# Joining the context and x feed-forward stages, and four unused products behind the last transposes of a stage

## The reference, cut to what matters

```python
def ffn_half(s, shift, scale, gate, g_pre, g_post, w_in, w_out):
    h = swiglu_2(modulate(rmsnorm_2(s, g_pre), shift, scale), w_in, w_out)
    return s + 0.5 * gate * rmsnorm_2(h, g_post)

xs = ffn_half(xs, mod_x[0], mod_x[1], mod_x[2], g[0], g[1], w_ff_in[l, 0], w_ff_out[l, 0])
cs = ffn_half(cs, mod_c[0], mod_c[1], mod_c[2], g[0], g[1], w_ff_in[l, 0], w_ff_out[l, 0])
hx = modulate(rmsnorm_2(xs, g[2]), mod_x[3], mod_x[4])
hc = modulate(rmsnorm_2(cs, g[2]), mod_c[3], mod_c[4])
```

## Time and profile before

| what | value |
|---|---|
| median of three runs | 2783.65 us |
| the profiled execution, its own time | 2785.72 us |
| span of the profile | 2783.7 us |
| PE matmul busy | 2589.7 us, 93% of the span |
| PE weight load, DVE, ACT, POOL busy | 74%, 66%, 52%, 3% |
| mean granted TensorE clock | 0.959 of full speed |
| `ff0c` and `ff0x` together, first L791 to the last L819's end | 1679.1 to 2083.6 us |

### The profile page before, as it was taken

The page is one execution under the profiler, slowest core; times in us unless marked ns, Lnnn a source line. Parts: engine busy times, 40 slices in busy tenths (PEclk is TensorE's granted clock), DMA queues, the critical chain, the costliest instruction groups (busy, mean ns, idle before and its releaser), DMA issues.

```text
span 2783.7 us, 34461 instructions
## 1 busy us (share of the span) xinstructions
PE 2589.7 (93%) x11943; PEld 2048.8 (74%) x11943; DVE 1823.6 (66%) x1799; ACT 1454.5 (52%) x1670; POOL 73.1 (3%) x46
## 2 busy tenths in 40 slices
PE   6889998877999999999999989999999989888998
PEld 5567886656878787888878777877874768667786
DVE  5445445556888989888888975445534565666544
ACT  4354444354767777776767764434432333446443
POOL 0000000041000000000000000000000000020000
PEclk9889999888999999999999999999999999999999
DMA  5756552657999999999999994554534325315551
GB/s 188 242 190 219 181 190 67 239 190 247 367 345 353 349 351 351 352 349 345 356 335 367 335 348 142 192 167 143 190 106 135 116 91 170 106 61 169 194 186 55
DMA packets 445869, 631.64 MB, mean 227 GB/s; under 512 B 17656, under 2 KB 345752, under 8 KB 445592
## 3 DMA queue, kind: packets, MB, share of 16 engines
q1 hardware_dynamic: 444920, 627.36, 67.1%
q0 software_dynamic: 864, 3.15, 0.3%
HBM read 629.40 MB, written 1.05 MB: 226 GB/s over the span
## 4 chain that ended last, share of the span: by engine, by line
PE 85%; DVE 8%; ACT 4%; issue 2%; DMA 1%; SPq 0%; DVEq 0%; ACTq 0%
PE ps L791 38%; PE ps L819 20%; PE ps L1145 5%; PE ps L725 5%; PE ps L1165 2%; PE ps L1077 2%; PE ps L913 1%; PE ps L804 1%; PE ps L853 1%; ACT Bs L1507 1%; DVE small L2508 1%; PE ps L1136 1%; PE ps L866 1%; ACT As L1459 1%; DVE Bs L2033 1%
## 5 line engine op out<-in xcount | busy, mean ns | idle before, releaser
L1996 DVE TENSOR_TENSOR As<-ringA,As 128x2048 fp32r<-128x2048 f32 x318 | 728.9, 2292 | 217.4 <-ACT As L1459 208.3
L791 PE MATMUL ps<-As,xgs 128*128 128x512 f32 x2688 | 665.9, 397 | 3.2 <-DVE As L1996 1.8
L819 PE MATMUL ps<-Bs,hds 128*128 128x512 f32 x2472 | 601.1, 396 | 24.0 <-DVE hds L2011 24.0
L1459 ACT ACTIVATE As<-ringA 128x2048 fp32r<-128x2048 f32 x318 | 608.0, 1912 | 20.4 <-DMA ringA<-in_dense_w_up 9.3
L791 PEld LDWEIGHTS ps<-As,xgs 128*128 128x128 f32 x2688 | 495.0, 188 | 113.1 <-issue 10.7
L819 PEld LDWEIGHTS ps<-Bs,hds 128*128 128x128 f32 x2472 | 472.6, 192 | 128.1 <-DVE hds L2011 23.1
L791 PE MATMUL ps<-As,xs 128*128 128x512 f32 x2160 | 522.9, 399 | 15.0 <-DVE hh L2027 8.1
L791 PEld LDWEIGHTS ps<-As,xs 128*128 128x128 f32 x2160 | 408.9, 191 | 104.9 <-DVE hh L2027 9.4
L2033 DVE TENSOR_TENSOR Bs<-ringB,Bs 128x2048 fp32r<-128x2048 f32 x159 | 364.5, 2292 | 154.6 <-ACT Bs L1507 154.0
L1507 ACT ACTIVATE Bs<-ringB 128x2048 fp32r<-128x2048 f32 x159 | 304.9, 1918 | 205.0 <-PE ps L819 204.8
L1480 ACT ACTIVATE hds<-ps 128x256 fp32r<-128x256 f32 x206 | 74.0, 383 | 322.8 <-PE ps L804 288.0
(11 more groups left out here) (342 smaller groups left out, 2419.9 us busy)
## 6 DMA issues: line engine op xcount, KB each, us to landing
ringA<-in_moe_w_gate SPq DMA_DIRECT2D x224, 512.0 KB, 4.5
ringA<-in_moe_w_up SPq DMA_DIRECT2D x224, 512.0 KB, 5.6
ringB<-in_moe_w_down SPq DMA_DIRECT2D x112, 1024.0 KB, 6.3
ringA<-in_w_ff_in SPq DMA_DIRECT2D x132, 512.0 KB, 4.7
ringA<-in_w_in SPq DMA_DIRECT2D x56, 1024.0 KB, 5.3
ringA<-in_w_ada SPq DMA_DIRECT2D x36, 1024.0 KB, 5.4
ringB<-in_w_ff_out SPq DMA_DIRECT2D x33, 1024.0 KB, 4.9
ringA<-in_dense_w_gate SPq DMA_DIRECT2D x28, 512.0 KB, 3.6
```

The source lines that it names most:

```text
L791: m = mm(ps[:, bank, :], lhs(l, tt, k), As[:, h, r, k % 4, :], start=k == 0 and n == 0, stop=k == KC - 1 and n == 2)
L819: m = mm(ps[:, 4 + 2 * tt + half, :], hds[:, buf, l, q, :], Bs[:, q, r, half * 512:(half + 1) * 512], start=first and q == 0 and n == 0, s ...
L1459: A(As[:, h, 0, :, :], ringA[:, (p["a"] + u) % 2, 4 * h:4 * h + 4, :], ACT.Copy).then_inc(A_high, 1)
L1996: V.tensor_tensor(As[:, h, 1, :, :], ringA[:, (p["a"] + u) % 2, 4 * h:4 * h + 4, :], f32(As[:, h, 0, :, :]), ALU.subtract).then_inc(A_spli ...
```

## The change

1. `ff0c` no longer drains (`drains=False`) and `ff0x` no longer leads (`leads=False`): the `turn` and `down` of the last context block are made inside the first block of `ff0x`, as between any two blocks.
2. The `norm("ff0x")` goes. x is squared and scaled tile by tile before the first block of `ff0c`, as before that block now; its transposes are made by the PE at the ends of blocks 1 and 2 of `ff0c` (eight each, one tile, L697's helper `turn_rows`, banks 2 and 3). ACT evacuates bank 2 ahead of its blocks 2 and 3, DVE bank 3 behind its blocks 1 and 2, four 128x128 instructions each. The PE waits for both (`x_rows_out`) before the `turn` of blocks 2 and 3. Ahead of ACT's block 3 and behind DVE's block 3, x is split into `hcTR` and `hTR`, which `ff0x` reads in the place of `xs`.
3. The context result leaves the accumulator in `context_end`: the squares and root ahead of ACT's block 1 of `ff0x`, `post` behind DVE's block 0, and the squares and scaling of the new `cs` ahead of ACT's block 2 and behind DVE's block 1. `down` of block 0 on the PE waits for `acc_free`, which `post` sends, as before.
4. In the last block of a two-tile stage that drains (`dense`, `ff0x`, `ff1`) the PE makes four float32 products of 128x128 by 128x512 (`idle_products(4)`) into bank 0 between the last `turn` and the last `down`. Nobody reads them.

```diff
+            def idle_products(n):
+                for _ in range(n):
+                    mm(ps[:, 0, :], ident, c1[:, 0:BW], start=True, stop=True)
...
-            def feed(p, lhs, T, e=0, ready=None, xsm=None, after=None, head=1, leads=True, drains=True, rows=None):
+            def feed(p, lhs, T, e=0, ready=None, xsm=None, after=None, head=1, leads=True, drains=True, rows=None, turns_free=None):
...
                     gu(i, u, 0)
+                    if turns_free and isinstance(i, int):
+                        turns_free(2 * i + u)
                     if not lead:
                         turn(*prev)
...
                     if last and drains:
                         turn(i, u)
+                        if T == 2:
+                            idle_products(4)
                         down(i, u)
...
-            feed(ph["ff0c"], split_stream, 2, ready=2 * ph["ff0c"]["xc"] + 1, xsm=xs_split)
-            norm(call["ff0x"])
-            feed(ph["ff0x"], split_stream, 2, ready=2 * ph["ff0x"]["xc"] + 1, xsm=xs_split)
+            def x_rows(n):
+                if n in (1, 2):
+                    for hf in range(2):
+                        turn_rows("ff0x", n - 1, hf)
+            def x_rows_out(n):
+                if n in (2, 3):
+                    pe.wait_ge(pn_hi, PN["ff0x"]["hi"] + n - 1)
+                    pe.wait_ge(pn_lo, PN["ff0x"]["lo"] + n - 1)
+            feed(ph["ff0c"], split_stream, 2, ready=2 * ph["ff0c"]["xc"] + 1, xsm=xs_split, head=2, drains=False, after=x_rows, turns_free=x_rows_out)
+            feed(ph["ff0x"], lambda l, tt, k: split_h[l][:, k, tt * P:(tt + 1) * P], 2, ready=2 * ph["ff0x"]["xc"] + 1, xsm=xs_split, leads=False)
...
ScalarE:
-            stats(call["ff0x"], [(x_ready, XR["final"])], lambda tt: x[:, tt, :], eps=1e-6)
+            for tt in range(TILES):
+                tile_stats("ff0x", tt, x, [(x_ready, XR["final"])])
+                tile_root(tt, tt + 1, D, 1e-6)
...
-            feed(ph["ff0c"], 2, ahead=True)
-            chunks(call["ff0x"], *mod_cols(0, 0), hT, parts=True)
-            acc_squares("ff0c", "ff0x")
-            stats(call["mixc"], [(x_ready, XR["ff0c"])], lambda tt: cs[:, tt, :], eps=1e-6)
-            feed(ph["ff0x"], 2)
+            def x_rows(n):
+                if n in (2, 3):
+                    tt = n - 2
+                    scale, shift = mod_cols(0, 0)
+                    act.wait_ge(pn_tp, PN["ff0x"]["tp"] + 2 * tt + 1)
+                    for j in range(4):
+                        last = A(hT[:, j, tt * P:(tt + 1) * P], ps[:, 2, j * P:(j + 1) * P], ACT.Identity, scale=scale(j), bias=shift(j))
+                    last.then_inc(pn_hi, 1)
+                if n == 3:
+                    act.wait_ge(pn_hi, PN["ff0x"]["hi"] + 2)
+                    act.wait_ge(pn_lo, PN["ff0x"]["lo"] + 2)
+                    for h in range(2):
+                        A(hcTR[:, 4 * h:4 * h + 4, :], hT[:, 4 * h:4 * h + 4, :], ACT.Copy).then_inc(xs_high, 1)
+            def context_end(n):
+                if n == 1:
+                    acc_squares("ff0c", pn_tp, PN["ff0x"]["tp"] + 4)
+                if n == 2:
+                    stats(call["mixc"], [(x_ready, XR["ff0c"])], lambda tt: cs[:, tt, :], eps=1e-6)
+            feed(ph["ff0c"], 2, ahead=True, head=2, drains=False, before=x_rows)
+            feed(ph["ff0x"], 2, head=2, leads=False, before=context_end)
...
VectorE:
-            scaled("ff0x", x)
-            feed(ph["ff0c"], 2, ahead=True)
-            chunks(call["ff0x"], dst=hT, parts=ph["ff0x"]["xc"], **mod_cols(0, 0))
-            post("ff0c_out", acc, 1, cs, ph["ff0c"]["f"] + 1)
-            dve.wait_ge(x_ready, XR["ff0c"])
-            scaled("mixc", cs)
-            feed(ph["ff0x"], 2)
+            for tt in range(TILES):
+                tile_scale("ff0x", tt, x, tt + 1)
+            def x_rows(n):
+                if n in (1, 2):
+                    tt, m = n - 1, mod_cols(0, 0)
+                    dve.wait_ge(pn_tp, PN["ff0x"]["tp"] + 2 * tt + 2)
+                    for j in range(4):
+                        last = V.tensor_scalar(hT[:, 4 + j, tt * P:(tt + 1) * P], ps[:, 3, j * P:(j + 1) * P], m["scale"](4 + j), m["bias"](4 + j), ALU.mult, ALU.add)
+                    last.then_inc(pn_lo, 1)
+                if n == 3:
+                    for h in range(2):
+                        dve.wait_ge(xs_high, 2 * ph["ff0x"]["xc"] + h + 1)
+                        V.tensor_tensor(hTR[:, 4 * h:4 * h + 4, :], hT[:, 4 * h:4 * h + 4, :], f32(hcTR[:, 4 * h:4 * h + 4, :]), ALU.subtract).then_inc(xs_split, 1)
+            def context_end(n):
+                if n == 0:
+                    post("ff0c_out", acc, 1, cs, ph["ff0c"]["f"] + 1)
+                if n == 1:
+                    dve.wait_ge(x_ready, XR["ff0c"])
+                    scaled("mixc", cs)
+            feed(ph["ff0c"], 2, ahead=True, head=2, drains=False, after=x_rows)
+            feed(ph["ff0x"], 2, head=2, leads=False, after=context_end)
```

More of the change, by code:

```diff
@@ L391, in build @@
         ffn("ff1", NB2)
-        NORMS = ["ff0c", "ff0x", "mixc", "mixx"]
+        NORMS = ["ff0c", "mixc", "mixx"]
         LATE = [(nm, n) for nm, nb in (("z", 6), ("hyo", 2), ("q2", 2), ("kv2", 4), ("gt2", 4), ("dao", 2), ("wo", 2)) for n in range(nb)]
@@ L399, in build @@
         XR = {n: i + 1 for i, n in enumerate(["out0", "dense", "out1", "moe", "final", "ff0c", "ff0x"])}
-        SQ = {n: i + 1 for i, n in enumerate(["ff0c", "final", "ff0x", "ff0c_out", "mixc", "ff0x_out", "mixx"])}
+        SQ = {n: i + 1 for i, n in enumerate(["ff0c", "final", "ff0c_out", "mixc", "ff0x_out", "mixx"])}
         PN, at = {}, dict(std=0, xn=0, tp=0, hi=0, lo=0)
-        for nm in ("attn0", "mix0", "ffn0", "attn1", "mix1", "ffn1", "ff1"):
-            mixed, plain = nm[:3] == "mix", nm == "ffn1"
+        for nm in ("attn0", "mix0", "ffn0", "attn1", "mix1", "ffn1", "ff0x", "ff1"):
+            mixed, plain = nm[:3] == "mix", nm in ("ffn1", "ff0x")
             PN[nm] = dict(at, mixed=mixed, plain=plain)
@@ L413, in rows_bank @@
         def rows_bank(nm, tt, hf):
-            return 4 + 2 * hf + tt if PN[nm]["mixed"] else 2 * tt + hf
+            return 4 + 2 * hf + tt if PN[nm]["mixed"] else 2 + hf if nm == "ff0x" else 2 * tt + hf
         COL_OF = {m: j for j, m in enumerate((0, 1, 3, 4, 6, 7))}
@@ L1703, in _, with acc_squares @@
             squares(lambda tt: x[:, tt, :], 1, 1e-5)
-            stats(call["ff0x"], [(x_ready, XR["final"])], lambda tt: x[:, tt, :], eps=1e-6)
-            def acc_squares(nm, c):
-                act.wait_ge(nt_tp, 8 * (call[c] + 1))
+            for tt in range(TILES):
+                tile_stats("ff0x", tt, x, [(x_ready, XR["final"])])
+                tile_root(tt, tt + 1, D, 1e-6)
+            def acc_squares(nm, *turned):
+                act.wait_ge(*turned)
                 act.wait_ge(down_done, ph[nm]["s"] + 2 * NB2)
                 squares(lambda tt: ps[:, 4 + 2 * tt:6 + 2 * tt, :].rearrange("p a b -> p (a b)"), 1, 1e-6)
-            feed(ph["ff0c"], 2, ahead=True)
-            chunks(call["ff0x"], *mod_cols(0, 0), hT, parts=True)
-            acc_squares("ff0c", "ff0x")
-            stats(call["mixc"], [(x_ready, XR["ff0c"])], lambda tt: cs[:, tt, :], eps=1e-6)
-            feed(ph["ff0x"], 2)
+            def x_rows(n):
[18 more added lines that the diff above has]
+            feed(ph["ff0x"], 2, head=2, leads=False, before=context_end)
             chunks(call["mixc"], *mod_cols(1, 1), hcT)
-            acc_squares("ff0x", "mixc")
+            acc_squares("ff0x", nt_tp, 8 * (call["mixc"] + 1))
             stats(call["mixx"], [(x_ready, XR["ff0x"])], lambda tt: x[:, tt, :], eps=1e-6)
```

## The result

| kernel | median of its runs, us | lowest to highest |
|---|---|---|
| before | 2783.75 (4 runs) | 2783.38 to 2784.52 |
| after | 2763.4 (4 runs) | 2761.81 to 2764.84 |

The ratio is 0.993, with a 95% interval of 0.9916 to 0.9944. The change is faster by 20.35 us; 28.7 were forecast, and 2763.4 lies above the range (2751 to 2761.5). The profiled execution of after took 2761.81.

What follows compares the result with a forecast made beforehand. The PE was taken as the bound, with 85% of the span. Joint 22.3 - 1.4 - 0.1 - 0.2 = 20.6, plus 8.1 from unused products, 28.7 us off 2783.65: 2755.0, range 2751 to 2761.5.

Steps and rivals of the forecast that it cites:

- The joint: From context block 10 to x block 0, the PE continues as between any two blocks; 20.6 us won, bounds 16.6 to 20.9.
- Removed, 22.3: Between `ff0c` and `ff0x`: waits, half-clock products and transposes lose 22.3 us over two blocks' pace, all removed.
- Transposes, 0.7 a tile: Ends of context blocks 1 and 2: eight transposes each add 0.7 us to the PE's path, 1.4 for both tiles.
- Evacuation 0, split of x 0: In `ff0c`: evacuating the transposes and splitting x on ACT and DVE are hidden, costing 0; failed evacuation cover at most 1.4 a tile.
- Context result, 0.1: First blocks of `ff0x`: taking out the context result barely delays `down` of block 0; 0.1 us, between 0 and 1.
- Rival C: Block 0 of `ff0x`: context result late, so `down` and the PE wait; costs 2 to 4 us, 2758; chance 0.06.
- Head of `ff0c`, 0.2: Start of `ff0c`: two roots instead of one make `hh` of block 0 later; 0.2 us, between 0 and 0.5.
- rival D: `ff0x` products reading `hcTR` and `hTR` get slower; a loss above 0.054 us each, 2792 at 0.07; chance 0.02.
- The unused products: Drains of `dense`, `ff0x`, `ff1`: four products keep full clock, so `down` takes 5.62; gains 2.15, 2.9, 3.0, together 8.1 us.
- rival A: In the three drains, unused products do nothing and `down` stays 8.5; 20.6 won, 2763.0; full or partial case, chance 0.14.
- Rival B: Clock falls behind the `ff0x` drain, slowing float32 tiles; about 3 us lost, 2758, at worst 2761; chance 0.12.
- the 3 I had allowed: Upper bound behind `dense`: if the clock also stays up into `in1`, up to 3 us more gained.

Runs made afterwards that it cites:

- GpSimd late: Kernel before, with GpSimd's gate rows held back until the experts' result is in x; median 2782.13 us, ratio 1.0005.
- the products alone: Kernel before plus four unused products in the drains of `dense`, `ff0x` and `ff1`, old joint kept; median 2777.49 us, ratio 0.9979.
- the other buffers: Kernel before, with x split into `hcTR` and `hTR` instead of `xs`, and `ff0x` reading those; median 2785.79 us, ratio 1.0012.
- after again: The changed kernel run once more with nothing edited; median 2764.02 us, ratio 0.9926 to before.
- the pad of 260 bytes: Changed kernel with 260 unused bytes a partition behind `hcTR`, moving all buffers behind it; 2760.46 us in one run.

## Why the prediction was wrong in size and right in kind

**The steps that failed.** The mechanism held; three terms of the sum were mis-sized. The products of `ff0x` on `hcTR` and `hTR` were put at nothing and cost 2.1 us. The losses made of half clock were taken from one execution as if fixed, which was 0.9 too much in the joint and 1.6 in the drains. The transposes cost 0.3 more than priced. Together 4.9 of the 8.35 us that are missing; 0.3 came back from costs that did not occur, and the rest, under 4 us, is open.

**The joint: 20.6 forecast, about 15 measured, 18.4 in the pair of profiles.** From the first `down` of `ff0c` to the last of `ff0x` before took 370.47 and after 352.04. The steps:

- *Removed, 22.3.* Right for the profile before, and for the kernel before with GpSimd late (370.40). Two other executions of the old joint lost 1.8 less: 368.68 with the products alone, and 370.46 - 1.74 = 368.72 with the other buffers. The mean of the four is 0.9 under the first. A loss made of a fallen clock was taken from one execution and treated as fixed.
- *Transposes, 0.7 a tile.* It was 0.87, twice: 0.34 less won. I had the four transposes from 0.32 "or a little more" and let the more go: 0.32 is when the next weight load began. The chain of before has the four at 0.44:

```profile
1715.53 0.44 PE ps L804 x4
```

- *Evacuation 0, split of x 0.* Right; no wait of the PE on `hT`.
- *Context result, 0.1.* Right: `down` of x block 0 follows without a wait. Rival C did not occur.
- *Head of `ff0c`, 0.2.* A wait of 0.73 for `hh`, but from the first gate and up to the first `down` it took 25.22 and 25.48 before. No loss.
- *`ff0x` on `hcTR` and `hTR`, not in the sum.* 1.74 us behind the `down` of its block 0, and 0.40 ahead of it, where gate and up of blocks 0 and 1 lie (34.20 across the joint against 33.80). The sentence that failed is "Nothing in the trace speaks for it", in rival D. I had checked the stationary buffers in a stage with other moving ones. The price was 4 ns a product, far from the 54 that would have turned the sign, but it was a real term, and 389 against 392 for `xgs` and `xs` stood in the trace of before.

In the profiles these leave 22.3 - 1.74 - 2.14 = 18.4, and with the mean of the four old executions 17.5; the 15.0 of the ratio has an interval of 10 to 19, which holds both. That the rest is scatter is argued, not shown.

**The unused products: 8.1 forecast, about 5.8 measured.** The mechanism held in every drain: `down` at 5.73 to 5.78, no delay, so rival A is out. The size did not: the slow `down` was 2.9 longer in one profile and 2.4 in the mean of 16 (8.13 - 5.74), so 2.4 + 2.4 + 1.7 = 6.5 by the forecast's own way of counting. `dense` itself came out as priced: 239.48 to 237.27 from its first gate and up to the next stage, 2.2, and 0.6 more in `in1`, a small piece of the 3 I had allowed.

**Rival B** did not occur either. Behind the drain of `ff0x` the PE does its 16 transposes with waits in between, and the float32 tiles follow; the windows of after:

```profile
2060.00:2066.00 6.00, 4.08 (x22) 2.53 (x21) 2.17 (x4) 3.31 (x7) 0.00 (x0) 1.00 0.00 0
2066.00:2072.00 6.00, 6.00 (x15) 2.66 (x14) 3.22 (x4) 2.65 (x4) 0.00 (x0) 1.00 0.01 1
```

The clock stays at 1.00, and the tiles up to the next stage take 72.26 (72.19 before). By the rule of the Trainium skill that I had quoted ("TensorE: Matmul & The Clock Gate", "Part 4: PE-mode transpose") it should have fallen; the measurement decides.

**Sum.** The pair of profiles differs by 24.4 (2783.7 to 2759.3): 27.1 in the stages that the change touches, close to the 28.7, and -2.7 elsewhere, where the attention won 4.9, the router lost 6.5, and 32 one-column products took 6.45 instead of 4.48. The change is not what lost there: from the end of `in1` to the last expert's gather it takes 1016.7 before and 1018.6 after, but 1018.9 in the kernel before with the other buffers. That the pair comes so near the forecast is partly luck, as all four slow drains of the profile before are among the long ones. The medians differ by 20.35, with an interval of 15.6 to 23.4.

With the terms as measured the sum is 28.7 - 2.1 - 0.9 - 1.6 - 0.3 + 0.3 = 24.1. That is still over the interval of the first measurement and inside that of after again (14.8 to 26.2). Whether the 3.7 us down to 20.35 are chance, no run shows. The range was too narrow because it treated all four slow drains as constants: with 7.04 instead of 8.5 for each, the same sum gives 28.7 - 4 x 1.5 = 22.7, and with the buffers 20.6.

## What to carry to other kernels

A loss made of half clock is a random variable: price it from several executions, or from every like place of one and its spread, before taking it as removable in full. A stage moved to other buffers can change the length of each matmul by how its two operands stand to each other in SBUF; check the pair, not the buffer. When a theory explains a run, go back to the earlier ones with it: the pad of 260 bytes had already spoken against distance. Work taken out of one engine's way falls somewhere else: look at what is there before counting the gain.

## What the runs showed of the hardware that I had not expected

- A 128x512 product had a median of 389, 392 or 396 to 398 ns depending on where in SBUF the stationary and the moving operand lie. Moving two buffers by some 100 KB made the slow pairs quicker (398 to 394, 396 to 392) and the quick ones slower (389 to 393); moving the others by 260 bytes did the second as well (389 to 396).
- A VectorE operation on 8 columns, 0.17 us alone, took 2.33 beside a GpSimd operation of 2.34 on 1024 columns; two of 1024 columns took 5.36 instead of 2.48.
- After the same idle time of 4.28 us, the same 24 products took from 7.04 to 8.63 us; after 2.36, 7.24 to 7.38; with two or four unused products in the gap, always 5.73 to 5.78.
